# Last stage of a streaming encoder step: one plain float32 matmul per product in place of three float32r products of split operands

## The reference, cut to what matters

```python
    h = h + jnp.concatenate([o_a, o_b], axis=-1) @ w_out      # (4224, 1024) @ (1024, 1024)
    e = rms_norm(p_i @ w_ple_proj, ple_norm_g)                # (4224, 256) @ (256, 1024)
    h = h + jax.nn.sigmoid(h @ w_ple_gate) * e                # (4224, 1024) @ (1024, 1024)
```

## Time and profile before

| | |
|---|---|
| median of three runs | 3681.2 us (3675.8 to 3689.92) |
| profiled execution | span 3678.1 us (the page gives no other time for it) |
| PE (matmul) busy | 3394.7 us, 92% of the span, 26606 instructions |
| PEld (weight loads) busy | 2899.7 us, 79% |
| DVE (VectorE) busy | 2181.8 us, 59% |
| ACT (ScalarE) busy | 1388.4 us, 38% |
| POOL (GpSimd) busy | 979.1 us, 27% |
| last stage | from 2768.7 us to the end, 909.4 us |

### The profile page before, as it was taken

The page is one execution under the profiler, slowest core; times in us unless marked ns, Lnnn a source line. Parts: engine busy times, 40 slices in busy tenths (PEclk is TensorE's granted clock), DMA queues, the critical chain, the costliest instruction groups (busy, mean ns, idle before and its releaser), DMA issues. The chain is left out here.

```text
span 3678.1 us, 69025 instructions
## 1 busy us (share of the span) xinstructions
PE 3394.7 (92%) x26606; PEld 2899.7 (79%) x26606; DVE 2181.8 (59%) x4410; ACT 1388.4 (38%) x2650; POOL 979.1 (27%) x1281
## 2 busy tenths in 40 slices
PE   7999999969998999998787567999997999999998
PEld 6999899957877888886777455888885888888887
DVE  7777687747987968761556455666664322323332
ACT  5555455533223323211555324666663111111111
POOL 3222122228996644400666400000000000000000
PEclk9999999979999999998999788999998999999999
DMA  5433333345337453434765543222225121212121
GB/s 157 116 105 105 107 108 112 89 149 152 127 103 227 133 158 103 123 105 142 250 209 191 135 139 124 73 76 85 73 70 175 56 74 56 69 60 68 61 69 36
DMA packets 320478, 420.06 MB, mean 114 GB/s; under 512 B 189923, under 2 KB 212739, under 8 KB 315574
## 3 DMA queue, kind: packets, MB, share of 16 engines
q1 hardware_dynamic: 320190, 416.17, 36.7%
HBM read 259.25 MB, written 159.46 MB: 114 GB/s over the span
## 5 line engine op out<-in xcount | busy, mean ns | idle before, releaser
L88 PE MATMUL b_psP<-b_w_hi,b_xT_hi 128*128 128x512 f32 x1320 | 518.9, 393 | 38.5 <-DVE b_xT_lo L1319 21.8
L89 PE MATMUL b_psP<-b_w_lo,b_xT_hi 128*128 128x512 f32 x1320 | 516.8, 391 | 0.0
L90 PE MATMUL b_psP<-b_w_hi,b_xT_lo 128*128 128x512 f32 x1320 | 516.5, 391 | 0.0
L88 PE MATMUL a_psG<-a_xT_hi,a_w_hi 128*128 128x256 f32 (+1 forms) x1536 | 453.6, 295 | 21.0 <-DVE a_xT_lo L668 19.5
L89 PE MATMUL a_psG<-a_xT_lo,a_w_hi 128*128 128x256 f32 (+1 forms) x1536 | 441.3, 287 | 0.0
L90 PE MATMUL a_psG<-a_xT_hi,a_w_lo 128*128 128x256 f32 (+1 forms) x1536 | 440.6, 287 | 0.0
L88 PEld LDWEIGHTS a_psG<-a_xT_hi,a_w_hi 128*128 128x128 f32 x1536 | 294.9, 192 | 42.6 <-DVE a_xT_lo L668 23.5
L88 PEld LDWEIGHTS b_psP<-b_w_hi,b_xT_hi 128*128 128x128 f32 x1320 | 249.8, 189 | 97.7 <-DVE b_xT_lo L1319 45.6
L685 DVE SCALAR_TENSOR_TENSOR a_act<-a_raw,a_taps,a_act 128x256 f32<-128x256 f32 x576 | 289.1, 502 | 20.6
L89 PEld LDWEIGHTS a_psG<-a_xT_lo,a_w_hi 128*128 128x128 f32 x1536 | 295.3, 192 | 0.0
L90 PEld LDWEIGHTS a_psG<-a_xT_hi,a_w_lo 128*128 128x128 f32 x1536 | 295.3, 192 | 0.0
(11 more groups left out here) (368 smaller groups left out, 7493.7 us busy)
## 6 DMA issues: line engine op xcount, KB each, us to landing
rows_b<-b_rows SPq DMA_DIRECT2D x165, 256.0 KB, 2.1
b_x_full<-xT SPq DMA_DIRECT2D x78, 512.0 KB, 4.3
qkvB<-a_act SPq DMA_DIRECT2D x16, 1536.0 KB, 5.4
d_conv_T<-qkvB SPq DMA_DIRECT2D x16, 1536.0 KB, 10.7
xT<-a_x_full SPq DMA_DIRECT2D x33, 512.0 KB, 3.6
h_mixed<-mixed SPq DMA_DIRECT2D x33, 512.0 KB, 4.0
out<-h_y SPq DMA_DIRECT2D x33, 512.0 KB, 2.9
a_x<-in_x_prompt SPq DMA_DIRECT2D x32, 512.0 KB, 4.4
```

The lines of the kernel that those rows point to most:

```text
L88: nc.tensor.matmul(out, x_hi, w_hi, start=first, stop=False)
L89: nc.tensor.matmul(out, x_hi, w_lo, start=False, stop=False)
L90: return nc.tensor.matmul(out, x_lo, w_hi, start=False, stop=last)
```

## The change

All of `combine` keeps one float32 buffer per operand (`w`, `mT`, `hT`, `pT`) instead of two float32r ones. Each of the 36 products per tile is one `nc.tensor.matmul` on float32 operands. The weights are loaded straight into `w`, all 18 loads in a row without waits, and TensorE waits for the load of each piece before its first use. ScalarE only copies `mT`, `hT` and `pT` out of PSUM; VectorE's subtractions are gone. The load of `mixed` for tile 2, which stood between weight pieces 10 and 11, stands behind piece 17. Earlier stages keep `matmul3` and are untouched; only their line numbers in the file move.

```diff
--- before.py
+++ after.py
@@ -88,23 +88,6 @@
...
-def load_weight(sp, k, stages, rows, there, lo_ok):
-
-    if k >= len(stages):
-        sp.wait_ge(lo_ok, k - len(stages) + 1)
-    sp.dma_start(stages[k % len(stages)], rows).then_inc(there[k], 16)
-
-
-def weight_hi(e, k, stages, hi, there, hi_ok):
-    e.wait_ge(there[k], 16)
-    e.activation(hi[k], stages[k % len(stages)], ACT.Copy).then_inc(hi_ok, 1)
-
-
-def weight_lo(v, k, stages, hi, lo, hi_ok, lo_ok):
-    v.wait_ge(hi_ok, k + 1)
-    v.tensor_tensor(lo[k], stages[k % len(stages)], hi[k].bitcast(F32), ALU.subtract).then_inc(lo_ok, 1)
...
@@ -3014,17 +2997,13 @@
...
-        w_hi = ph.sb("h_w_hi", [P, WEIGHTS, D], F32R)
-        w_lo = ph.sb("h_w_lo", [P, WEIGHTS, D], F32R)
+        w = ph.sb("h_w", [P, WEIGHTS, D])
         mixed = [ph.sb(f"h_mixed{i}", [P, MIX]) for i in range(2)]
         x = ph.sb("h_x", [P, D])
         p_in_rows = [ph.sb(f"h_p{i}", [P, s.PLE]) for i in range(2)]
-        mT_hi = ph.sb("h_mT_hi", [P, MT, P], F32R)
-        mT_lo = ph.sb("h_mT_lo", [P, MT, P], F32R)
-        hT_hi = ph.sb("h_hT_hi", [P, KT, P], F32R)
-        hT_lo = ph.sb("h_hT_lo", [P, KT, P], F32R)
-        pT_hi = ph.sb("h_pT_hi", [P, PT, P], F32R)
-        pT_lo = ph.sb("h_pT_lo", [P, PT, P], F32R)
+        mT = ph.sb("h_mT", [P, MT, P])
+        hT = ph.sb("h_hT", [P, KT, P])
+        pT = ph.sb("h_pT", [P, PT, P])
...
@@ -3108,10 +3082,9 @@
                     load_x(a)
                 load_p(a)
             for k in range(WEIGHTS):
-                load_weight(sp, k, stages, weight(k), w_in, w_lo_ok)
-                if k == PT + MT:
-                    sp.wait_ge(mT_ps, 1)
-                    load_m(Tile(2, 0, 1, 2))
+                sp.dma_start(w[:, k, :], weight(k)).then_inc(w_in[k], 16)
+            sp.wait_ge(mT_ps, 1)
+            load_m(Tile(2, 0, 1, 2))
             sp.wait_ge(h_ok, HALVES)
             load_x(Tile(1, 1, 0, 2))
 
@@ -3148,27 +3121,20 @@
 
         @block.scalar
         def _(sc):
-            def split_weight(k):
-                weight_hi(sc, k, stages, parts_hi, w_in, w_hi_ok)
-
-            def split_m(a):
+            def take_m(a):
                 sc.wait_ge(mT_ps, a.t + 1)
-                sc.activation(mT_hi[:, :, :], psT[:, :].rearrange("p (k n) -> p k n", k=MT), ACT.Copy).then_inc(m_hi, 1)
-
-            split_m(Tile(0, 0, 0, 2))
-            for k in range(MT):
-                split_weight(k)
-            split_m(Tile(1, 1, 0, 2))
-            for k in range(MT, WEIGHTS):
-                split_weight(k)
+                sc.activation(mT[:, :, :], psT[:, :].rearrange("p (k n) -> p k n", k=MT), ACT.Copy).then_inc(mT_ok, 1)
+
+            take_m(Tile(0, 0, 0, 2))
+            take_m(Tile(1, 1, 0, 2))
 
             def iteration(a):
                 sc.wait_ge(hT_ps, a.t + 1)
-                sc.activation(hT_hi[:, :, :], psT[:, :].rearrange("p (k n) -> p k n", k=KT), ACT.Copy).then_inc(h_hi, 1)
+                sc.activation(hT[:, :, :], psT[:, :].rearrange("p (k n) -> p k n", k=KT), ACT.Copy).then_inc(hT_ok, 1)
                 sc.wait_ge(pT_ps, a.t + 1)
-                sc.activation(pT_hi[:, :, :], psE[:, 0:s.PLE].rearrange("p (k n) -> p k n", k=PT), ACT.Copy).then_inc(p_hi, 1)
+                sc.activation(pT[:, :, :], psE[:, 0:s.PLE].rearrange("p (k n) -> p k n", k=PT), ACT.Copy).then_inc(pT_ok, 1)
                 if within(a, 2):
-                    split_m(a.plus(2))
+                    take_m(a.plus(2))
                 sc.wait_ge(e_ps, a.t + 1)
                 if not a.first():
                     sc.wait_ge(e_sq, a.t)
@@ -3185,11 +3151,13 @@
         def _(pe):
             pe.wait_ge(filled, 2)
 
-            def product(ps, hi, lo, first_k, kt, done, each_half):
+            def product(ps, xT, first_k, kt, done, each_half, landing=False):
                 for n in range(HALVES):
                     for k in range(kt):
-                        last = matmul3(nc, ps[:, half(n)], hi[:, k, :], lo[:, k, :], w_hi[:, first_k + k, half(n)],
-                                       w_lo[:, first_k + k, half(n)], k == 0, k == kt - 1)
+                        if landing and n == 0:
+                            pe.wait_ge(w_in[first_k + k], 16)
+                        last = nc.tensor.matmul(ps[:, half(n)], xT[:, k, :], w[:, first_k + k, half(n)],
+                                                start=k == 0, stop=k == kt - 1)
                     if each_half or n == HALVES - 1:
                         last.then_inc(done, 1)
 
@@ -3200,16 +3168,15 @@
                 last.then_inc(mT_ps, 1)
 
             def mix(a):
-                pe.wait_ge(m_lo, a.t + 1)
-                product(psH, mT_hi, mT_lo, 0, MT, h_ps, True)
+                pe.wait_ge(mT_ok, a.t + 1)
+                product(psH, mT, 0, MT, h_ps, True)
 
             transpose_m(Tile(0, 0, 0, 2))
-            pe.wait_ge(m_lo, 1)
+            pe.wait_ge(mT_ok, 1)
             for k in range(MT):
-                pe.wait_ge(w_lo_ok, k + 1)
+                pe.wait_ge(w_in[k], 16)
                 for n in range(HALVES):
-                    last = matmul3(nc, psH[:, half(n)], mT_hi[:, k, :], mT_lo[:, k, :], w_hi[:, k, half(n)],
-                                   w_lo[:, k, half(n)], k == 0, k == MT - 1)
+                    last = nc.tensor.matmul(psH[:, half(n)], mT[:, k, :], w[:, k, half(n)], start=k == 0, stop=k == MT - 1)
                     if k == MT - 1:
                         last.then_inc(h_ps, 1)
             transpose_m(Tile(1, 1, 0, 2))
@@ -3217,7 +3184,7 @@
             def iteration(a):
                 pe.wait_ge(h_ok, HALVES * (a.t + 1))
                 if within(a, 1):
-                    pe.wait_ge(m_lo, a.t + 2)
+                    pe.wait_ge(mT_ok, a.t + 2)
                 for k in range(KT):
                     last = nc.tensor.transpose(psT[:, k * P:(k + 1) * P], h[a.b][:, k * P:(k + 1) * P], ident[:, :])
                 last.then_inc(hT_ps, 1)
@@ -3228,18 +3195,14 @@
                 last.then_inc(pT_ps, 1)
                 if within(a, 1):
                     mix(a.plus(1))
-                pe.wait_ge(h_lo, a.t + 1)
+                pe.wait_ge(hT_ok, a.t + 1)
                 if within(a, 2):
                     transpose_m(a.plus(2))
-                pe.wait_ge(p_lo, a.t + 1)
-                if a.first():
-                    pe.wait_ge(w_lo_ok, PT + MT)
-                product(psE, pT_hi, pT_lo, MT, PT, e_ps, False)
-                if a.first():
-                    pe.wait_ge(w_lo_ok, WEIGHTS)
-                else:
+                pe.wait_ge(pT_ok, a.t + 1)
+                product(psE, pT, MT, PT, e_ps, False, a.first())
+                if not a.first():
                     pe.wait_ge(sig_ok, HALVES * a.t)
-                product(psG, hT_hi, hT_lo, PT + MT, KT, g_ps, True)
+                product(psG, hT, PT + MT, KT, g_ps, True, a.first())
 
             pipeline(pe, iteration)
 
@@ -3249,18 +3212,6 @@
                 v.sem_inc(stored[b], 16)
             v.sem_inc(e_ok, HALVES)
             v.wait_ge(consts, 16)
-
-            def split_weight(k):
-                weight_lo(v, k, stages, parts_hi, parts_lo, w_hi_ok, w_lo_ok)
-
-            def low(lo, hi, ps, there, done, a):
-                v.wait_ge(there, a.t + 1)
-                k = lo.shape[1]
-                v.tensor_tensor(lo[:, :, :], ps.rearrange("p (k n) -> p k n", k=k), hi[:, :, :].bitcast(F32), ALU.subtract)\
-                    .then_inc(done, 1)
-
-            def split_m(a):
-                low(mT_lo, mT_hi, psT[:, :], m_hi, m_lo, a)
 
             def residual(a):
                 v.wait_ge(x_in, 16 * (a.t + 1))
@@ -3270,21 +3221,11 @@
                     v.wait_ge(h_ps, HALVES * a.t + n + 1)
                     v.tensor_tensor(h[a.b][:, half(n)], psH[:, half(n)], x[:, half(n)], ALU.add).then_inc(h_ok, 1)
 
-            split_m(Tile(0, 0, 0, 2))
-            for k in range(MT):
-                split_weight(k)
             residual(Tile(0, 0, 0, 2))
-            split_m(Tile(1, 1, 0, 2))
-            for k in range(MT, WEIGHTS):
-                split_weight(k)
 
             def iteration(a):
-                low(hT_lo, hT_hi, psT[:, :], h_hi, h_lo, a)
-                low(pT_lo, pT_hi, psE[:, 0:s.PLE], p_hi, p_lo, a)
                 if within(a, 1):
                     residual(a.plus(1))
-                if within(a, 2):
-                    split_m(a.plus(2))
                 v.wait_ge(e_rstd, a.t + 1)
                 if not a.first():
                     v.wait_ge(y_ok, HALVES * a.t)
```

More of the change, by code:

```diff
@@ L3043, in combine @@
         w_in = [ph.sem(f"h_w_in{k}") for k in range(WEIGHTS)]
-        w_hi_ok = ph.sem("h_w_hi_ok")
-        w_lo_ok = ph.sem("h_w_lo_ok")
         m_in = [ph.sem(f"h_m_in{i}") for i in range(2)]
@@ L3048, in combine @@
         p_in = [ph.sem(f"h_p_in{i}") for i in range(2)]
-        mT_ps, m_hi, m_lo = ph.sem("h_mT_ps"), ph.sem("h_m_hi"), ph.sem("h_m_lo")
```

(7 more changed lines are left out.)

## The result

The changed kernel takes 3873.45 us in the median of three runs (3869.62 to 3883.23), the kernel before 3681.2 us: a ratio of 1.0525, 95% interval 1.0492 to 1.0558. The forecast was 3877 us.

A forecast was written before the change was run, and what follows sets the result against it. The prediction took TensorE alone to set the last stage's pace: +208.9 us for the products less 13.5 us at the start and end is +195.4 us, from 3681.2 to about 3877 us, range 3860 to 3908 us.

The forecast's parts named there:

- A plain product is two records 0.428 us apart: On TensorE a plain float32 product takes two matmul records, 0.856 us, against 0.680 us for three float32r matmuls.
- +208.9 us for 1188 products: Last stage, TensorE: each of 1188 products costs 0.176 us more, all on the path, +208.9 us.
- -13.5 us at the start and the end: Last stage: four savings in TensorE's waits, in the first tiles and the last tile, together -13.5 us.
- (a): Stage start: the first product begins when the first weight has landed, not when it is split, -2.4 us.
- (b): Transposes of `h` for tile 0 no longer wait for the `lo` part of tile 1's `mT`, -1.2 us.
- (c): Tile 0: the 6.45 us stall goes as ScalarE no longer splits 10 weights before `hT`'s copy; with slow clock -8.1 us.
- (d): Last tile: TensorE no longer waits for `pT_lo` from DVE, only for ScalarE's copy, -1.8 us.
- The slack of `mixed`: Tile 2's load behind all 18 weights lands nine us before TensorE asks; loads half as fast would cost some 12 us.
- Cheaper records: Rival: each plain record costs a float32r matmul's 0.2267 us, -269 us, about 3399 us; chance of faster 0.04.
- weight loads laid bare: Rival: 2376 weight loads of 0.19 us exposed on TensorE, +451 us, about 4328 us; chance, fully or in part, 0.03.
- an overhead of 8 to 13 ns a record: Rival: long rows of plain records have L2073's or float32r's overhead, 3893 to 3906 us; chance of 5 to 15 ns 0.22.
- a time within 0.5%: Rival: products cost the same, 0.34 us a record, or start and end hide the difference; chance 0.01.

The follow-up runs named there:

- hT first: The kernel before with the splits of tile 0's hT and pT moved ahead of those of weight pieces 10 to 17 on ScalarE and VectorE: 3677.1 us, ratio 0.9984.

## Why the prediction was right

- **TensorE alone bounds the stage.** Right. PE was busy in all of the middle after the change as before, and with one matmul of each product taken away (two products) the tile shrank by 8.16 us, just 36 x 0.227.
- **A plain product is two records 0.428 us apart.** Right: 0.4291 us over 32 records, two records per product, 592 ns long. It rested on a single distance between two records of the same shape. The 1061 ns median of that line would have given a product of twice the time, and the narrow products of L2102 one that is shorter than before. The part over the 1024 cycles is 2.4 ns a record. The Trainium skill, "TensorE: Matmul & The Clock Gate", section "Wait — 56ns, not 53.3ns?", gives about 2.5 ns per warm matmul; an estimate that counts them once per record over 1024 cycles is 429.2 ns, what the trace shows. The estimate in the prediction had counted them four times a product.
- **+208.9 us for 1188 products.** A tile became 32.87 - 26.50 = 6.37 us longer, 0.177 us a product, times 33 tiles is +210.2.
- **-13.5 us at the start and the end.** (a) from the stage's first load to the first product 12.7 us before, 10.4 after: -2.3 for -2.4. (b) 2.5 us of waiting became 1.2: -1.3 for -1.2. (c) no wait and no slow clock at tile 0's transposes of `mixed` and `psE`: -8.1 as forecast; that this was the order is shown by "hT first". (d) 3.08 us became 1.3: -1.8. Together 210.2 - 13.5 = 196.7, the stage measured +196.4. That the two agree so closely is in part luck: "hT first" shows slow stretches, worth 1.5 us each, that came behind the same waits in one profiled run and not in another. The profile of the kernel before had, behind the stage's first `psH`, only the one that (c) counts.
- **The slack of `mixed`.** Right in the changed kernel, 10 us for the nine forecast; with the loads doubled the wait was 9.7 us, where the prediction had "some 12".
- **The rivals.** Cheaper records fell to the 0.4291 us; weight loads laid bare fell to the same number, which leaves 2.4 ns over the record's 1024 cycles where a load takes 190; an overhead of 8 to 13 ns a record did not come at 512 columns, and was 5 ns at 128; a time within 0.5% fell to the +5.25%.

The medians of three differ by 192 us, the two profiled spans by 203 us and their stages by 196 us. The unchanged part ahead moves by several microseconds from run to run; it was 7 us longer in the profile after.

## What to carry to other kernels

Count the cycles that a product takes on TensorE, not its instructions: one plain float32 matmul of 512 columns was two records of two cycles per column, 0.858 us, so it costs more than three float32r matmuls at 0.227 us, and would be the cheaper one only against four (0.907 us). When TensorE is busy without a gap, work saved on VectorE and ScalarE is worth only what stands in the gaps at the start and the end; here 13 us against 210. To price an operation that the kernel does not have yet, look for the same shape elsewhere in its own trace, at the same clock and width of the array, and take the distance between starts.

## What the runs showed of the hardware beyond that

- A float32r matmul of 512 columns starts every 0.227 us, a bfloat16 one every 0.216 us; the weight loads take 188 against 98 ns, and 190 in plain float32. The Trainium skill, "TensorE: Matmul & The Clock Gate", section "Weight-path perf modes — Fast Weight Load (FWL) and DoubleRow", has fast weight load only for types other than FP32; the loads of float32r ran at float32's duration.
- A product of one float32r and two bfloat16 matmuls took 0.677 us with the types alternating and 0.6625 us with them sorted within a half of 8 products; the single spacings add up to 0.659.
- Plain float32 records of 128 columns took 0.1116 us in rows of 128, with loads of 192 ns each, and 0.115 us in the short rows of L2073.
- Behind the same wait TensorE went on at full rate in one profiled run and at half rate in another. After the 2.5 us wait for `mT_lo`, `psH` of tile 1 had starts 0.23 us apart in the kernel before and 0.43 us apart in "hT first"; after the 3.1 us wait for `pT_lo`, `psE` of the last tile had 0.23 us in the kernel before and 0.43 us in parts of it in "hT first". Each such place was worth 1.5 us.
